# RWKV-7 outputs with tokens on partitions, group norm along the free axis

## The reference, cut to what matters

```python
def _wkv_step(S, inp):
    r, w, k, v, kk, b = inp
    sa = jnp.einsum('bhvk,bhk->bhv', S, -kk)
    S = S * w[:, :, None, :] + sa[..., :, None] * b[:, :, None, :] + v[..., :, None] * k[:, :, None, :]
    y = jnp.einsum('bhvk,bhk->bhv', S, r)
    return S, y
...
    y = jnp.moveaxis(y, 0, 1)
    mu = jnp.mean(y, axis=-1, keepdims=True)
    var = jnp.mean(jnp.square(y - mu), axis=-1, keepdims=True)
    y = (y - mu) * lax.rsqrt(var + LNX_EPS) * hp(lnx_g) + hp(lnx_b)
    y = y + jnp.sum(r * k * r_k.astype(f32), axis=-1, keepdims=True) * v
    out = y.reshape(B, T, A_W).astype(xm.dtype) * g
```

## Time and profile before

| | us |
|---|---|
| median of 3 runs | 1865.8 (1865.79 to 1867.06) |
| profiled execution | 1865.56 |
| its span, first to last instruction | 1863.7 |
| busy: TensorE / VectorE / ScalarE | 1544.5 / 661.3 / 306.3 |

### The profile page before, as it was taken

How to read it: one execution, slowest core, us unless ns; L and a number is a source line. 1 busy time by engine, 2 the same in 40 slices (tenths; PEclk the granted TensorE clock), 3 DMA queues, 4 the chain that set the end, 5 groups by cost and what they waited for, 6 DMA issues and landing times.

```text
span 1863.7 us, 24676 instructions
## 1 busy us (share of the span) xinstructions
PE 1544.5 (83%) x8916; PEld 883.2 (47%) x8916; DVE 661.3 (35%) x1297; ACT 306.3 (16%) x711; POOL 64.6 (3%) x103
## 2 busy tenths in 40 slices
PE   7999999999999999999996685666757667576666
PEld 4676767676767676676752231222312223122112
DVE  6747575757575757410121120111201111020014
ACT  2323232323232323100112000000000000000003
POOL 1000000101010101000000000000000000000000
PEclk9999999999999999999997887888878788787878
DMA  7223232323232323373589999999999999999996
GB/s 293 103 103 110 96 121 83 121 83 121 83 121 83 121 83 121 123 303 145 212 373 428 428 427 428 428 428 429 428 428 429 428 429 429 428 429 428 428 407 243
DMA packets 72802, 509.31 MB, mean 273 GB/s; under 512 B 20497, under 2 KB 25745, under 8 KB 38833
## 3 DMA queue, kind: packets, MB, share of 16 engines
q1 hardware_dynamic: 72706, 508.56, 67.6%
q0 software_dynamic: 48, 0.12, 0.0%
HBM read 498.83 MB, written 9.82 MB: 273 GB/s over the span
## 4 chain that ended last, share of the span: by engine, by line
PE 51%; DMA 33%; DVE 11%; issue 2%; SPq 2%; DVEq 1%; ACT 0%; ACTq 0%
DMA arena<-w_up 21%; PE ps_PJ L734 18%; DMA arena<-w_down 11%; DVE arena L1463 11%; PE ps_C L1085 8%; PE ps_PJ L934 7%; SPq L562 1%; PE ps_C L1122 1%; PE ps_SB L1122 1%; DMA arena<-cst 1%; PE ps_YB L1122 1%; PE ps_C L796 1%; PE ps_PJ L1027 1%; PE ps_RT L1122 1%; PE ps_C L805 1%
## 5 line engine op out<-in xcount | busy, mean ns | idle before, releaser
L734 PE MATMUL ps_PJ<-arena 128*128 128x320 f32 x1792 | 536.6, 437 | 0.0
L1085 PE MATMUL ps_C<-arena 128*32 128x512 f32 x2048 | 286.5, 722 | 176.0 <-DMA arena<-w_gate 111.6
L734 PEld LDWEIGHTS ps_PJ<-arena 128*128 128x128 f32 x1792 | 324.7, 190 | 124.7 <-issue 17.9
L1463 DVE TENSOR_TENSOR arena<-arena,ps_PJ 128x512 f32<-128x512 f32 (+4 forms) x115 | 74.0, 643 | 596.2 <-PE ps_PJ L1034 476.3
L1085 PEld LDWEIGHTS ps_C<-arena 128*32 128x32 f32 x2048 | 79.7, 130 | 375.9 <-issue 373.5
L1463 DVE TENSOR_TENSOR arena<-arena 128x320 f32<-128x320 f32 (+13 forms) x313 | 171.8, 549 | 74.4 <-ACTq L424 34.1
L1191 ACT ACTIVATE arena<-arena 32x160 f32<-32x160 f32 (+9 forms) x353 | 147.2, 417 | 291.1 <-DVEq L424 101.5
L1191 ACT ACTIVATE arena<-ps_C 128x128 f32<-128x128 f32 (+4 forms) x69 | 27.8, 403 | 931.6 <-PE ps_C L1085 530.1
L934 PE MATMUL ps_PJ<-arena 128*128 128x320 f32 x512 | 142.4, 433 | 1.0 <-DVEq L424 1.0
L934 PEld LDWEIGHTS ps_PJ<-arena 128*128 128x128 f32 x512 | 95.5, 190 | 40.2 <-issue 3.3
L1463 DVE TENSOR_TENSOR arena<-ps_PJ,arena 128x512 f32<-128x512 f32 x32 | 22.1, 692 | 255.8 <-PE ps_PJ L1027 255.6
(11 more groups left out here) (184 smaller groups left out, 1183.4 us busy)
## 6 DMA issues: line engine op xcount, KB each, us to landing
arena<-w_down SPq DMA_DIRECT2D x63, 2048.0 KB, 20.3
arena<-w_gate SPq DMA_DIRECT2D x61, 2048.0 KB, 20.2
arena<-w_up SPq DMA_DIRECT2D x61, 2048.0 KB, 20.2
arena<-win SPq DMA_DIRECT2D x59, 1024.0 KB, 4.8
arena<-w_out SPq DMA_DIRECT2D x16, 1024.0 KB, 6.8
arena<-w_gate SPq DMA_DIRECT2D x6, 1024.0 KB, 8.0
arena<-xT SPq DMA_DIRECT2D x8, 640.0 KB, 7.0
arena<-s_ret SPq DMA_DIRECT2D x8, 512.0 KB, 3.7
```

The lines of the kernel that those rows point to most:

```text
L734: last = mm(pj(j)[:, 0:T], wt[j % NSLOT][:, kt, :], hT[:, kt, :], start=kt == 0, stop=kt == KT - 1)
L1085: last = mm((GB, UB)[u][h * CAP:(h + 1) * CAP, :], xg[:, kt, h * CAP:(h + 1) * CAP], w[h](k), start=kt == 0, stop=kt == KT - 1)
L1463: ins = build(*args)
```

## The change

The y products swap their sides: the chunk's columns become the weights (64 columns), and the state or the value rows move (128 columns). So y lies in PSUM with 128 partitions = two chunks of 64 tokens, and 384 columns = two prompt halves and the sample tokens, each with two heads of 64 features. The two products with QA in us get a 32-column weight `seq_y`. The norm is then over 64 neighbouring columns: VectorE reduces each of the six groups of columns to a mean (mean6), subtracts it, ScalarE squares each group with an accumulated sum (var6) and takes the root of six columns, VectorE inverts them and multiplies (pr). TensorE turns the result back to feature rows with three transposes (new step yt), and pw needs two operations. The steps mu and va leave TensorE's list.

```diff
@@ PLAN, LATE
-    "q": "@v ax am -va u0 | cv us0 | | k1 i1 | zs1 xb mb | j1 pd | ds1 | k2 i2",
-    "kr": "@q | rqa j2 zs2 xk | | k3 i3 rqb mx | ds2 | j3 xv | | k4 i4",
+    "q": "@v ax am u0 | cv us0 | | k1 i1 | zs1 xb mb | j1 pd | ds1 -pr | k2 i2",
+    "kr": "@q | rqa j2 zs2 xk | -yt | k3 i3 rqb mx | ds2 | j3 xv | | k4 i4",
...
-LATE = {"u1": 1, "s1": 2, "u2": 1, "r2": 2, "a2": 2, "s2": 2, "r3": 2, "a3": 2, "s3": 4, "mu": 3, "va": 7}
+LATE = {"u1": 1, "s1": 2, "u2": 1, "r2": 2, "a2": 2, "s2": 2, "r3": 2, "a3": 2, "s3": 12, "yt": 2}
@@ TensorE, once at the start
                     pe.wait_ge(sum_done, 1)
+                    mm(psum["YB"][:, T:3 * P], ones, t1[:, 0:HD], start=True, stop=True)
                     mm(psum["YB"][:, 0:T], ones, t1, start=True, stop=True).then_inc(sem("mean_full"), 1)
@@ TensorE, steps s0 to s3
-                    yb = psum["YB"][:, c * C:(c + 1) * C]
+                    yb = psum["YB"][halves[c % 2], c // 2 * P:c // 2 * P + P]
                     if c > 0:
-                        mm(yb, S, AR[:, c, P:192], start=True, stop=False)
-                    mm(yb, SA, GM[:, c, 0:C], start=c == 0, stop=False)
-                    last = mm(yb, tok[:, 0, c, :], GM[:, c, 256:320], start=False, stop=True)
+                        mm(yb, AR[:, c, P:192], S, start=True, stop=False)
+                    mm(yb, GM[:, c, 0:C], SA, start=c == 0, stop=False)
+                    last = mm(yb, GM[:, c, 256:320], tok[:, 0, c, :], start=False, stop=True)
@@ TensorE, step us
-                    yb = psum["YB"][:, TP:T]
-                    mm(yb, SAs, GM[:, NC, P:192], start=True, stop=False)
-                    mm(yb, tokS[:, 0, :], GM[:, NC, 320:384], start=False, stop=False)
+                    yb = psum["YB"][halves[0], 2 * P:3 * P]
+                    mm(yb, GM[:, NC, P:192], SAs, start=True, stop=False)
+                    mm(yb, GM[:, NC, 320:384], tokS[:, 0, :], start=False, stop=False)
                     for g in range(2):
-                        mm(yb[:, 32 * g:32 * g + 32], QA[:, g, :], seq_rows[:, :, 16:24], start=False, stop=g == 1)
+                        mm(yb[32 * g:32 * g + 32, :], seq_y, QA[:, g, :], start=False, stop=True)
@@ TensorE, steps mu and va; step yt
-                elif s == "mu":
+                elif s == "yt":
                     wait_done(pe, "yin", p)
-                    mm(b[:, 0:T], hsum, y, start=True, stop=True).then_inc(full(s), 1)
-                elif s == "va":
-                    wait_done(pe, "ysq", p)
-                    mm(b[:, 0:T], hsum, yq, start=True, stop=True).then_inc(full(s), 1)
+                    nc.tensor.transpose(b[:, 0:P], yc[:, 0:P], ident)
+                    nc.tensor.transpose(b[:, P:TP], yc[:, P:TP], ident)
+                    nc.tensor.transpose(b[:, TP:T], yc[halves[0], TP:3 * P], ident[halves[0], 0:HD]).then_inc(full(s), 1)
@@ ScalarE, steps va and mu
-                elif s == "va":
-                    wait_filled(act, s, p)
-                    A(yq, bank(s)[:, 0:T], ACT.Sqrt, bias=eps[:, 1:2], scale=1.0 / HD).then_inc(free(s), 1)
...
-                    A(yq, y, ACT.Square).then_inc(done("ysq"), 1)
+                    for g in range(6):
+                        A(sq64, y_groups[:, g, :], ACT.Square, accum_out=var6[:, g:g + 1])
+                    A(var6, var6, ACT.Sqrt, bias=eps[:, 1:2], scale=1.0 / HD).then_inc(done("ysq"), 1)
@@ VectorE, once at the start
+            CP(seq_y.rearrange("p (c t) -> p c t", c=4), seq_rows[:, :, 16:24])
@@ VectorE, steps my, mu, pr, pw
-                    CP(y, psum["YB"][:, 0:T]).then_inc(free("y"), 1)
...
-                    STT(y, bank(s)[:, 0:T], -1.0 / HD, y, ALU.mult, ALU.add).then_inc(free(s), 1)
...
+                    yb = psum["YB"][:, 0:3 * P].rearrange("p (g j) -> p g j", j=HD)
+                    RED(mean6, yb, AX_X, ALU.add)
+                    TSC(mean6, mean6, 1.0 / HD, None, ALU.mult)
+                    TT(y_groups[:, :, :], yb, mean6[:, :, None].broadcast_to([P, 6, HD]), ALU.subtract).then_inc(free("y"), 1).then_inc(done("ydev"), 1)
...
-                    RECIP(yq, yq)
+                    wait_done(dve, "ysq", p)
+                    RECIP(var6, var6)
+                    TT(y_groups[:, :, :], y_groups[:, :, :], var6[:, :, None].broadcast_to([P, 6, HD]), ALU.mult).then_inc(done("yin"), 1)
...
-                    STT(y, y, scol(p, "lnx_g"), yq, ALU.mult, ALU.mult)
-                    STT(y, y, scol(p, "lnx_b"), bsv, ALU.add, ALU.add)
-                    TT(yT[:, p, :], y, gg, ALU.mult).then_inc(done("y"), 1)
+                    wait_filled(dve, "yt", p)
+                    STT(bsv, bank("yt")[:, 0:T], scol(p, "lnx_g"), bsv, ALU.mult, ALU.add).then_inc(free("yt"), 1)
+                    STT(yT[:, p, :], bsv, scol(p, "lnx_b"), gg, ALU.add, ALU.mult).then_inc(done("y"), 1)
```

More of the change, by code:

```diff
@@ L88 @@
 }
-LATE = {"u1": 1, "s1": 2, "u2": 1, "r2": 2, "a2": 2, "s2": 2, "r3": 2, "a3": 2, "s3": 4, "mu": 3, "va": 7}
-UNSEEN = ("xb", "xk", "xv", "mb", "mx", "mv", "ts", "pk", "ck", "cr", "cv", "e3", "lo", "sq", "pc", "pe", "p1", "p2", "ps", "b1", "b1k", "b1l", "b2a", "b2b", "ax", "am", "u0", "us0", "vt", "mk", "pd", "pr", "pw", "rqa", "rqb", "rka", "rkb", "th", "mr", "mg", "my")
+LATE = {"u1": 1, "s1": 2, "u2": 1, "r2": 2, "a2": 2, "s2": 2, "r3": 2, "a3": 2, "s3": 12, "yt": 2}
+UNSEEN = ("mu", "xb", "xk", "xv", "mb", "mx", "mv", "ts", "pk", "ck", "cr", "cv", "e3", "lo", "sq", "pc", "pe", "p1", "p2", "ps", "b1", "b1k", "b1l", "b2a", "b2b", "ax", "am", "u0", "us0", "vt", "mk", "pd", "pr", "pw", "rqa", "rqb", "rka", "rkb", "th", "mr", "mg", "my")
 def schedule(now, late):
@@ L175, in build_program @@
         kp = c0
-        y, yq = sb(T), sb(T)
+        yc, sq64, seq_y = sb(3 * P), sb(HD), sb(BK)
+        mean6, var6 = sb(6), sb(6)
+        y_groups = yc.rearrange("p (g j) -> p g j", j=HD)
         wcs = sb(NC)
@@ L971, in _ @@
             wait_freed(pe, "u2", PAIRS - 1)
-            wait_freed(pe, "va", PAIRS - 1)
+            wait_freed(pe, "yt", PAIRS - 1)
             wait_freed(pe, "a3", PAIRS - 1)
@@ L1320, in step @@
                     if isinstance(p, int):
-                        A(yq[:, 0:1], eps[:, 0:1], ACT.Sqrt)
+                        A(sq64[:, 0:1], eps[:, 0:1], ACT.Sqrt)
                     wait_done(act, "ydev", p)
-                    A(yq, y, ACT.Square).then_inc(done("ysq"), 1)
+                    for g in range(6):
+                        A(sq64, y_groups[:, g, :], ACT.Square, accum_out=var6[:, g:g + 1])
+                    A(var6, var6, ACT.Sqrt, bias=eps[:, 1:2], scale=1.0 / HD).then_inc(done("ysq"), 1)
                 elif s == "tkk":
```

7 lines of the change are left out of this document (removed), and 4 rows, old and new, of tables (BANKS, PLAN).

## The result

| | before | after |
|---|---|---|
| median of the runs of the comparison (us) | 1865.9 (1865.6 to 1867.6, 7 runs) | 1872.4 (1871.9 to 1874.1, 7 runs) |
| profiled execution: time, span (us) | 1865.56, 1863.7 | 1873.86, 1872.1 |
| period of a pair, zw to zw, mean of pairs 2 to 6 (us) | 91.75 | 92.65 |
| start of the last output product ahead of the first transposition L956 (us) | 791.5 | 797.5 |

The ratio after to before is 1.0033, with an interval of 1.0023 to 1.0043: slower by a third of a per cent, 6.5 us, where 6.7 was forecast. Seven periods of +0.9 and a shorter tail put this output product 6.0 us later; everything behind it takes as long as before to within 0.5 us (medians less these starts: 1074.4 and 1074.9).

What follows compares the result with a forecast made beforehand. TensorE was taken to bound the eight pairs and output projection, the DMA the experts. Seven pairs at +0.96 (+6.7), +0.57, +0.2 and -0.8 made +6.7 on 1865.6: 1872.3 us, range 1866.5 to 1878.5.

Steps and rivals of the forecast that it cites:

- the excursions: TensorE going to narrower weights and back in the y steps: 0.34 us each, ends 0 and 0.35; forecast's chance 0.64.
- s0, s1: Y steps where TensorE is not waiting: each 0.34 us a pair longer from the narrower weights.
- s2, s3: Y steps between r2 and g4: their 0.68 us goes into the 0.67 wait at g4, so they cost nothing.
- yt: New step of three transposes on TensorE: 0.40 us a pair, range 0.33 to 0.68 if the 64-row third costs extra.
- mu and va: Products removed from TensorE, 1.35 us a pair: 0.35 comes back, ends 0 and 0.81, because VectorE's masks follow later.
- The y products: Swapped products in s0 to s3 and us: moving cost unchanged; 64-column weights add 0.34 us a step, us 0.23.
- the sign to look for: In the profile after, s1 from first y product to next projection takes 1.46 us instead of 1.12.
- the wait of 1.00: Rest of the 1.35 us removed from TensorE turns into waits for VectorE at g3, i1 and zs1.
- Free width: Rival: 64-wide products in the y steps cost nothing extra; 1861.5 us, or 1856 with halves side by side; chance 0.08 for both.
- All of mu and va back: Rival: TensorE regains the whole 1.35 us a pair; time 1865.6, no change, or 1869.1 halfway; chance 0.20.
- ScalarE late: Rival: squares at 0.75 us hold the copies of v and ax; k1/i1 wait up to 1.2 more; 1880; chance 0.08.
- Start and tail: Before the first projections +0.2 us, pair 0's s0 and us +0.57, after pair 7 -0.8.

Runs made afterwards that it cites:

- e1: Changed kernel with 128-column instead of 64-column weights in the y products of s0 to s3, half the recurrence's output left out: 1867.3 us, ratio 1.0005.
- e4: Changed kernel with the first state product moved between the y products of s0 to s3, so two changes to 64-column weights a step: 1880.2 us, ratio 1.0075.
- e8: Changed kernel with 128-column weights in s0, s1 and us and three full transposes in yt, s2 and s3 still narrow: 1862.8 us, ratio 0.9984.
- e6: Kernel before without the product mu, VectorE's operation behind it kept and reading y itself: 1858.9 us, ratio 0.9964.
- e7: Kernel before without the product va, ScalarE taking the root of the squares themselves: 1866.0 us, ratio 0.9998.
- e9: Changed kernel with k1, i1 and the steps behind them up to j5 one projection part (four passes) later: 1865.4 us, ratio 0.9994.
- e2: Changed kernel with my and the squares moved from tile v to behind i2 in tile q, pr and yt following later: 1878.2 us, ratio 1.0064.

## Why the prediction came out right, step by step

The total was right (1872.3 forecast, 1872.4 measured), and the forecast's case, the excursions, is the one that happened. Not every term was.

| term, a pair (us) | predicted | measured |
|---|---|---|
| s0, s1 | +0.34 each | +0.33 each |
| us | +0.23 | +0.21 |
| s2, s3 | 0 (0.68 into g4's wait) | 0 (0.45 into g4's wait) |
| yt | +0.40 | +0.62 |
| mu and va | -0.35 | -0.65 (mu -0.81, va -0.54, i1 +0.70) |
| ms | 0 | +0.07 |
| sum | +0.96 | +0.91 |

**The y products** were priced from L966, at 0.35 for an excursion, with 0 as the other end if L956 were the pattern. e1 and e4 show the price by itself, taken away and doubled. It is 0.09 of standstill at either side, a weight load of 0.05 that stands exposed behind the first, and one of 0.10 behind the second. Only the sign to look for was put wrong: s1 from its first y product to the next projection is 1.34, not 1.46, because the first 0.09 lies ahead of that product. The Trainium skill, page TensorEngine Tiling (Array Packing), section Key Properties, says that a change of tiling mode drains TensorE; the trace agrees, with 0.09 of standstill at either side. The same page of the Trainium skill recommends, under When to Use Tiling, the swap with twofold column tiling for a short moving side. Here the swap cost 0.33 a step: one half alone was in use, and the moving side hadn't limited the old products (five products took 1.12 with 64 columns moving in three of them, and 1.12 with 128 in all of them, e1). Both halves side by side weren't tried.

**yt** was mis-sized, 0.40 for 0.62. I took the third transposition to be nearer to L956, which loses nothing. But L956's third has all 128 rows and 64 columns, as a window on it alone shows (the earlier trace rows merge the three under the shape of the first):

```profile
912.75 0.27 PE L956 MATMUL ps_C<-arena 128*64 128x128 f32 x1
```

yt's third has 64 rows (64*128), and that is an excursion, 0.29, which e8 takes away by reading 128. My upper end, 0.68, had it; my choice did not. The Trainium skill, Gotcha 2 of the same page, excludes column tiling for an fp32 transposition, and lists no such exclusion for rows; the trace agrees with both: 64 columns lost nothing, 64 rows 0.29.

**mu and va**: the rule I used, that the gain is what g3's mask is earlier, was right, and its size wrong, 0.35 for 0.65. I had VectorE reach g0 0.33 later, and it was 0.09. My's new operations add 0.85 (from the end of s3's update to g4's mask 1.83, 248.22 to 250.05; before 0.98, 246.44 to 247.42) where I had summed 1.17: each operation was sized well, but I counted two gaps of 0.15 which the trace hardly has (0.03 and 0.04). The old mu operation gives back 0.76, from g4's mask to g0's, where I had 0.84. With 0.09 in the place of 0.33 the same sum gives 0.59 back; 0.65 was measured. What the prediction did not see is the order of the two: mu comes back whole, va not at all (e6, e7), and the wait of 1.00 that it spread over g3, i1 and zs1 is one of 0.70 at i1 alone. zs1 and g3 show no new wait. Its list of waits lacks the one at i1, which the kernel before has already: 0.35 from k1 to i1, where the least in these runs is 0.20 (e9). So TensorE's work between g3 and i1 could be taken away without gain. And the picture behind it, a my that holds the masks up, is good for 0.15 to 0.17 only (e2); the rest is the way from g3's last product through VectorE's queue to the spread, 5.5 to 5.7 us in every version looked at, which va had covered.

The two errors, yt 0.22 too low and the return 0.30 too low, have opposite effects on the sum. That the total hit is in part luck: either alone would have put it 1.5 to 2.1 us off.

**The rivals.** Free width: refuted by e1 and e4. All of mu and va back: halfway true, mu was (e6). ScalarE late: its six squares take 0.38 each, and it is idle when the ax copies can start. **Start and tail.** The first zw comes 0.08 later, not 0.2; the time from it to the next zw grows by 0.84, which holds the s1 of tile k too (0.57 and 0.34 were forecast). From the end of s3 of pair 7 to the output products that follow yt 8.64 passed, where 8.6 was forecast. **The 0.07 at ms** appears in e6 and e7 too, where nothing near it was changed; its cause stays open.
